# Output projection finished tile of tokens by tile of tokens, with the work behind it reordered

## The reference

```python
xl = xl + g1l * (jnp.concatenate([a_lat, b_lat, c_lat], axis=-1) @ w_out[layer])
h2l = (rms_norm(xl, norm2_gain[layer]) * (1.0 + sc2l) + sh2l).reshape(-1, D_MODEL)
xl = xl + g2l * hierarchical_moe(h2l, *moe_w).reshape(xl.shape)
```

## Time and profile before

| | |
|---|---|
| median of 3 runs | 2271.33 us (2271.33, 2271.38, 2256.76) |
| the profiled execution's own time | 2259.08 us |
| its span, first to last instruction | 2257.2 us |
| mean granted TensorE clock | 0.937 |
| this stage, of that span | 1580.7 to 1640.0 us |
| PE busy over the span | 1987.9 us (88%) |
| DVE, ACT busy over the span | 1441.3 us (64%), 1100.1 us (49%) |

### The profile page before, as it was taken

One profiled execution on the slowest core, in us unless ns is written; L12 is line 12 of the kernel. 1 busy time (PEld: TensorE's weight loads), 2 busy tenths in 40 slices (PEclk: granted clock), 3 DMA queues, 4 the chain that ended last, 5 costly groups with the idle time before them and its releaser, 6 DMA issues. The chain is left out here.

```text
span 2257.2 us, 37023 instructions
## 1 busy us (share of the span) xinstructions
PE 1987.9 (88%) x15254; PEld 1670.8 (74%) x15254; DVE 1441.3 (64%) x1794; ACT 1100.1 (49%) x1334; POOL 146.7 (7%) x151
## 2 busy tenths in 40 slices
PE   4698899899788899899959895898899999999997
PEld 3586677899577677799848664786778788787785
DVE  0264445786355444688547939765788788788886
ACT  0253343655253343466346433222567677676773
POOL 0000000000000000000004613720000000000000
PEclk9799999999899879899979997899899999999998
DMA  8775364545266237444342120000689899799895
GB/s 320 284 240 164 103 224 141 218 178 185 104 219 217 94 126 248 166 157 183 131 136 91 56 73 11 14 20 11 229 297 378 298 350 378 270 369 337 311 380 219
DMA packets 153800, 447.54 MB, mean 198 GB/s; under 512 B 10032, under 2 KB 12720, under 8 KB 151088
## 3 DMA queue, kind: packets, MB, share of 16 engines
q1 hardware_dynamic: 153648, 445.41, 55.2%
HBM read 444.33 MB, written 1.05 MB: 197 GB/s over the span
## 5 line engine op out<-in xcount | busy, mean ns | idle before, releaser
L212 DVE TENSOR_TENSOR me_wlow<-me_w,me_whigh 128x2048 fp32r<-128x2048 f32 (+1 forms) x203 | 451.8, 2247 | 108.0 <-ACT me_whigh L207 107.8
L207 ACT ACTIVATE me_whigh<-me_w 128x2048 fp32r<-128x2048 f32 (+1 forms) x203 | 380.1, 1884 | 134.3 <-PE ps L220 126.3
L218 PE MATMUL ps<-me_whigh,me_xhigh 128*128 128x512 f32 x512 | 207.1, 404 | 12.0 <-PEq L119 12.0
L218 PE MATMUL ps<-up_xhigh,ffn_whigh 128*128 128x256 f32 x704 | 201.8, 287 | 8.1 <-DVE ffn_wlow L212 6.5
L220 PE MATMUL ps<-me_whigh,me_xlow 128*128 128x512 f32 x528 | 208.4, 395 | 0.0
L219 PE MATMUL ps<-me_wlow,me_xhigh 128*128 128x512 f32 x512 | 201.9, 394 | 0.0
L219 PE MATMUL ps<-up_xlow,ffn_whigh 128*128 128x256 f32 x704 | 201.0, 286 | 0.0
L220 PE MATMUL ps<-up_xhigh,ffn_wlow 128*128 128x256 f32 x704 | 200.9, 285 | 0.0
L212 DVE TENSOR_TENSOR ffn_wlow<-ffn_w,ffn_whigh 128x2048 fp32r<-128x2048 f32 (+1 forms) x72 | 149.3, 2110 | 60.8 <-ACT ffn_whigh L207 60.6
L212 DVE TENSOR_TENSOR mix_wlow<-mix_w,mix_whigh 128x1024 fp32r<-128x1024 f32 (+2 forms) x116 | 140.3, 1213 | 69.5 <-ACT mix_whigh L207 69.2
L207 ACT ACTIVATE ffn_whigh<-ffn_w 128x2048 fp32r<-128x2048 f32 (+1 forms) x72 | 123.2, 1759 | 47.8 <-PE ps L220 47.8
(11 more groups left out here) (665 smaller groups left out, 4212.5 us busy)
## 6 DMA issues: line engine op xcount, KB each, us to landing
me_w<-w_exp_gate SPq DMA_DIRECT2D x34, 2048.0 KB, 9.8
me_w<-w_exp_up SPq DMA_DIRECT2D x34, 2048.0 KB, 10.2
me_w<-w_exp_down SPq DMA_DIRECT2D x32, 2048.0 KB, 10.1
mix_w<-w_mix SPq DMA_DIRECT2D x108, 512.0 KB, 4.2
mix_aside<-ada_w SPq DMA_DIRECT2D x96, 512.0 KB, 4.3
ffn_w<-ffn_w_up SPq DMA_DIRECT2D x20, 2048.0 KB, 7.7
ada_w<-ada_first SPq DMA_DIRECT2D x12, 2048.0 KB, 22.6
ffn_w<-ffn_w_down SPq DMA_DIRECT2D x8, 2048.0 KB, 7.9
```

The costliest lines, as they stand in the source:

```text
L207: return nc.scalar.activation(high, x, ACT.Copy)
L212: return nc.vector.tensor_tensor(low, x, high.bitcast(F32), ALU.subtract)
L218: nc.tensor.matmul(out, lh, rh, start=start, stop=False)
```

## The change

1. `TAIL = 4`: the last four row tiles of the projection, not the last two, go tile of tokens by tile of tokens. `w_done` counts accordingly.
2. The second gate row's product on PE moves from ahead of the router to between the two parts of `back_pe`, and its copy on ACT behind the copies of h2T's turned rows.
3. Splits of the first expert weights move: on ACT the second and third go behind the first squares; on DVE the first goes behind the first residual, the second behind the second token tile's diagonal, the third behind the clearing of the banks.
4. The planned times of residual, norm, `h2T`, logits and `back_pe` change to fit.

```diff
+        TAIL = 4
...
         def out_pe(pe):
-            for kt in range(KD - 2):
+            for kt in range(KD - TAIL):
...
-            yield 5.3 + 2.72 * (KD - 2)
+            yield 5.3 + 2.72 * (KD - TAIL)
             pe.wait_ge(y_low, KD)
             for t in range(TT):
                 for n in range(2):
-                    for kt in (KD - 2, KD - 1):
+                    for kt in range(KD - TAIL, KD):
                         pe.wait_ge(w_low, kt + 1)
                         mm = product(t, n, kt)
                     mm.then_inc(w_done, 1)
 
         def ended(t, n):
-            return 3 + 2 * t + n + 1
+            return (KD - TAIL) // 2 + 2 * t + n + 1
...
             row_products(0, (0, 1))
-            yield 29.5
+            yield 36.3
             pe.wait_ge(row_made, 2)
             pe.wait_ge(scaled, 4)
             row_products(1, (2, 3))
...
-            yield 36.0
+            yield 40.0
             for n in range(2):
                 act.wait_ge(row_done, 3 + n)
...
-                    yield 24.3 + 2.7 * t + 0.7 * n
+                    yield 21.6 + 5.4 * t + 0.7 * n
                     dve.wait_ge(w_done, ended(t, n))
...
-                yield 31.2 + 4.0 * t
+                yield 29.2 + 4.9 * t
...
-                    yield (34.0, 37.4)[t] + 0.5 * n
+                    yield (34.3, 36.4)[t] + 0.5 * n
...
         def first_act(act):
             for i in range(AHEAD):
-                yield (19.6, 21.6, 25.2)[i]
-                act.wait_ge(w_done, i + 1)
+                yield (19.6, 26.0, 29.5)[i]
+                act.wait_ge(w_done, i + 1 if i < 2 else ended(1, 1))
...
         def first_dve(dve):
             for i in range(AHEAD):
-                yield (21.6, 23.6, 33.4)[i]
+                yield (24.4, 31.2, 41.9)[i]
```

More of the change, by code:

```diff
@@ L3802, in residual_dve @@
                 for n in range(2):
-                    yield 25.7 + 2.7 * t + 0.6 * n
+                    yield 23.0 + 5.4 * t + 0.6 * n
                     dve.wait_ge(scaled, 2 * t + n + 1)
@@ L3811, in norm_act @@
                     i = 2 * t + n
-                    yield 26.3 + 2.7 * t + 0.6 * n
+                    yield 23.6 + 5.4 * t + 0.6 * n
                     act.wait_ge(added, i + 1)
@@ L3817, in norm_act @@
                         .then_inc(squared, 1)
-                yield 27.8 + 2.7 * t
+                yield 25.1 + 5.4 * t
                 act.wait_ge(summed, t + 1)
@@ L3823, in norm_dve @@
             for t in range(TT):
-                yield 27.6 + 2.7 * t
+                yield 24.9 + 5.4 * t
                 dve.wait_ge(squared, 2 * t + 2)
@@ L3829, in norm_dve @@
                                                op0=ALU.add, op1=ALU.add).then_inc(summed, 1)
-                yield 28.3 + 2.7 * t
+                yield 25.6 + 5.4 * t
                 dve.wait_ge(rooted, t + 1)
@@ L3840, in norm_pe @@
             for t in range(TT):
-                yield 29.0 + 3.0 * t
+                yield 27.2 + 4.6 * t
                 pe.wait_ge(diag_made, t + 1)
@@ L3850, in fixed_dve @@
                 for kt in range(KH):
-                    yield 30.0 + 3.0 * t + 0.2 * kt
+                    yield 28.2 + 4.6 * t + 0.2 * kt
                     dve.wait_ge(x_turned, 2 * t + 1)
@@ L3861, in fixed_act @@
                 for kt in range(KH, KD):
-                    yield 30.2 + 3.0 * t + 0.2 * kt
+                    yield 28.4 + 4.6 * t + 0.2 * kt
                     act.wait_ge(x_turned, 2 * t + 2)
```

## The result

The changed kernel's median is 2274.65 us over 20 runs (2259.41 to 2283.39); the kernel before, timed beside it, has 2267.95 (2256.76 to 2276.24, 20 runs). The ratio is 1.0033, with a 95% interval of 1.0017 to 1.0048: the change costs about 7.5 us of 2268 (3.9 to 10.9). Forecast was +3.9 us, a change too small to be told from none at 1%. That and the sign came true; the size was about half of what was measured.

What follows compares the result with a forecast made beforehand. PE was taken to bound most of the program, but the router's chain through DVE to set the stage's end. +1.75 and +2.19 made +3.9 us on 2271.33, so 2275.2 us; range 2258 to 2281.

Steps and rivals of the forecast that it cites:

- steps 1, 2: Projection's tail and first token tile's norm: sums end 2.72 us apart, first turn follows without a gap, 1.64 us earlier.
- step 3: ACT after the first turn: third high split delays last square and h2T row; second turn 0.85 us later than before.
- step 4: Second token tile's h2T and logits: second low split replaces the third behind a later turn; biased logits 0.32 us earlier.
- step 5: PE before the rank product: gate row stands ahead, start +1.75 us including -0.32; full clock could save up to 0.65.
- step 6: DVE before the chain's second part: the third low split stands ahead of it, adding 2.19 us.
- the second rival: PE's clock falls early, at about 1618, between the turns: slower by up to 9.1 us in all; chance 0.18.
- the signs given: Marks expected in the changed profile, such as biased logits 4.3 us after the second turn and a 63.2 us stage.

Runs made afterwards that it cites:

- the filler: Changed kernel plus sixteen matmuls that nobody reads, between the first token tile's logits on PE; ratio to before 1.0000 (0.9973 to 1.0027).
- gate row early: Changed kernel with the second gate row's eight matmuls back ahead of the first logits; ratio 1.0027 (1.0000 to 1.0054).
- high split later: Changed kernel with ACT's third high split moved from the first h2T rows to behind the second token tile's root; first expert matmul at 61.00 us, no ratio given.
- all three moves: Changed kernel with gate row early, third low split in DVE's wait for the rank, and high split later; ratios to before 0.9969, then 0.9997.

## Why the prediction was right, and where it wasn't

Right were that the change can't be told from none at 1%, the sign, and the order's part. Between marks, in the two first profiles:

| from | to | forecast | measured |
|---|---|---|---|
| start | first matmul of the projection | 0 | -0.61 |
| there | first turn (steps 1, 2) | -1.64 | -2.96 |
| first turn | second turn (step 3) | +2.49 | +1.99 |
| second turn | biased logits (step 4) | -1.17 | +2.09 |
| biased logits | rank read (step 5) | +2.07 | +3.67 |
| rank read | second part (step 6) | +2.19 | +2.20 |
| second part | first expert matmul | 0 | +0.01 |
| | sum | +3.9 | +6.4 |

- Start to the first matmul of the projection: this varies from 7.6 to 8.7 us over the fourteen profiles, which have the same work up to there. The -0.61 lies within that and says nothing of the change.
- Steps 1 and 2: the turn follows the projection without a gap, as said. The gain beyond -1.64, 1.3 us, goes to the 1.5 us that the low clock at the projection's start cost before.
- Step 3: 7.37 us from turn to turn, 7.9 forecast. Half of the 0.5 lies in ACT's rows ahead of the last square (5.6 us after the first turn, 5.9 forecast), half in the square and the chain of sum, root and diagonal behind it (1.8 against 2.0). That the third high split on ACT makes the second turn late is shown: without it 5.58.
- Steps 4 and 5 are the ones that failed, and both for the one reason that was the second rival: the clock was forecast at 1.00 until the rank product and at 0.50 there, and was the other way round. At full clock the working holds: with the filler, second turn to biased logits is 4.39 us (4.3 forecast), and from there to the rank read 4.20 (4.87 forecast with the rank product at half clock, less the 0.65 that was its other bound). So steps 4 and 5 were sized right as order and wrong as clock: together 5.76 us against 0.90.
- Step 6: 2.20 against 2.19.

Of the signs given, those of steps 1, 2, 3 and 6 came. Those of steps 4 and 5 didn't: 7.57 us from the second turn to the biased logits, not 4.3, a wait of 4.94 us for the rank product, not about 3, and a stage of 65.7 us, not 63.2.

The second rival, given 0.18 and up to +9.1, was the case. It was named "early fall, at about 1618", which is where it came. Its price by the rows at half clock, up to 5.2 us on top, met 5.4, but partly by luck. It had nothing for the second token tile's logits, which cost some 1.4 us more than with the filler, and 0.95 for the second turning back, which ran at full clock again (1.04 us). What was wrong was its chance: I noted that the new order leaves 16 short records where 48 stood, and then took the clock from where it fell before. The sign that the text named as wrong, a fall before 1625, is what the profile shows. The rows of the table add up: the forecast 3.9, plus 4.9 in steps 4 and 5, less 1.9 ahead of the first turn and 0.5 in step 3, is the 6.4 measured.

The range held the time, and would have done so without the second rival, as the spread of before's runs is most of it: 2271.38 + 5 is 2276.4. The median of the changed kernel, 2274.65, is near the forecast 2275.2 by luck, because the base was high by 3.4: before's median of 20 is 2267.95, not the 2271.33 of three runs.

The rule of the Trainium skill (TensorE: Matmul & The Clock Gate, "Why this matters for your kernels"), to leave no long idle gap between bursts of matmuls, pointed the right way. The trace agrees that waits of PE brought the clock down, but the longest gap doesn't sort the cases: the clock fell with gaps of 1.16 and 1.41 us (changed) and with none over 0.98 us (gate row early), and held with one of 1.17 us (high split later) and with 0.47 us at most (all three moves). Where the line lies is open.

## What to carry to other kernels

When a short step is taken out of PE's queue because it "isn't wanted yet", ask what PE will do in its place: if the answer is to wait in small pieces, the clock's fall can cost more than the step did. Putting the step back isn't always the cure: here the clock still fell with the gate row back in its place, and held once the long split was out of the rows that PE waited for. Where an order is written out by hand, place each movable piece where its engine already waits for longer than the piece takes; here the same split cost 2.2 us behind a memset, nothing in a wait that was longer than it, and 1.4 us once another move had made that wait shorter. And where timing scatters by more than the effect, marks within one stage over two or three profiles tell what the median can't.

## What the runs showed of the hardware

- A stretch of 5.6 us with PE busy for 3.0, in which no gap was over 1.4 us, saw the granted clock go from 1.00 to 0.50 in 3 of 3 profiles. Filled to 5.49 of 5.68 us it stayed at 1.00 in 2 of 2.
- After such a fall the clock stayed at 0.50 for some 13 us in the changed kernel, though PE was busy for 7.42 of 7.70 us in the middle of it, and for some 3 us in the kernel with the low split moved, whose PE queue is the same. In those three profiles steady work of short matmuls didn't bring the clock back sooner.
- 16 records of a 128x128 float32 product took 3.78 us with the clock at 0.50 throughout (second turn of the changed kernel), and 1.95 to 2.05 us at 1.00. Eight transpositions of 128x128 took 1.95 us at 0.50 and 1.04 at 1.00.
